# Three-pass projection in the second layer of block 1, with modulation chunks loaded elsewhere

## The chip, the cores and the metric

The kernel runs on one core of a Trainium2 chip, in float32. Its time is the device time of one launch in microseconds. TensorE is called PE here, VectorE DVE, ScalarE ACT and GpSimd POOL, as the profile's rows do; SP is the engine whose queue issues most DMAs.

## The reference

The model is two blocks in a row. What matters here is the first, which has two layers, each on 256 rows of context and 256 latent rows of width 1024:

```python
for l in range(DEPTH):
    mod_lat = silu_c @ w_ada[l] + b_ada[l]
    mod_ctx = silu_cc @ w_ada[l] + b_ada[l]
    x, ctx = _layer(x, ctx, mod_lat, mod_ctx, tabs, g_norm[l], w_in[l], ...)
...
xn = _rms_norm(x, g_norm) * (1 + sc[:, None]) + sh[:, None]
cn = _rms_norm(ctx, g_norm) * (1 + sc_c) + sh_c
(au, av, az, bq, bk, bv, bz, cq, ck, cv, co, cz, cg) = _split_proj(xn @ w_in)
```

`w_in` is 1024 x 3344 in each layer. Of the context the second layer needs only the columns of keys, values and gates. Behind the projection come a gated MLP branch, attention and an mLSTM, then `w_out`. The second block (a dilated attention, a forgetting attention, each with a mixture of experts) takes its own modulation from a vector, `mod = silu(c_2) @ w_ada_2[i] + b_ada_2[i]`, 6144 values for each of its layers. Those values depend on no row of x, so their weights (12 chunks of 512 columns, 2 MB each) may be used early: in block 1, where the kernel has room.

## The kernel before

**Weights.** All large weights pass through a ring of six buffers of 1 MB (`RING`, `SLOT`), filled by SP in the order of `ring_items()` (L96). A chunk of 512 columns is two items, one for each half of the 1024 rows. Item n goes where item n - 6 was, and SP waits for that one's last reader; it issues in order, so one item that cannot go yet holds all behind it.

**The projection** takes `w_in` in seven chunks of columns, `CHUNKS`: 272 columns first, then six of 512. There are four row tiles of 128 rows (0 and 1 context, 2 and 3 latent) and eight blocks of 128 along the 1024.

In the **first layer** `project_split` computes each product in three passes: the rows are kept as a rounded part `XH` and a remainder `XL`, the weights as `WH` and `WL`, and PE adds XH x WH, XH x WL and XL x WH (L3021 to L3023). POOL writes both weight parts, block by block (`WH` has four places, `WL` overwrites the ring's item). PE goes block by block over four tiles, so a chunk holds four PSUM banks until its last block; ACT then evicts them (`evict`, L2213), with a table load ahead where the chunk needs Gelu, Silu or Sigmoid. `MODS_BEHIND[0]` says which chunks of block 1's own modulation stand behind which chunk of the projection: PE multiplies them (`ada_rows`), DVE copies the result (`ada_copy`, L2354), PE gathers it into columns (`ada_row_cols`, L2936) and DVE adds the bias (`ada_sums`). While chunk 6 runs, PE does three pieces of side work, behind blocks 1, 3 and 5 (`SIDE_CHUNK`); each waits for a small write of DVE (`d2p`), the first for the one at L2645.

In the **second layer** `project` multiplies the rows `XT` by the ring's weights as they are (L3003), in full precision, tile by tile, 16, 256 or no columns for the context (`CTX_LAST`). `norm_by_tile` has PE wait for all eight blocks of XT before. Between the chunks DVE reduces seven chunks of the second block's modulation (3 to 9, `MODS_BEHIND[1]`): eight steps each on 128 x 512, L2321 and L2323, and PE turns each into columns with four small products (L2909). The work that follows a chunk (`post`: gates, the q/k norm, the layer norm of the values, the mLSTM's heads) is DVE's and ACT's, and starts when the chunk is evicted. Chunks 0 to 2 of that modulation come in the first layer's attention, 10 and 11 in the second's.

**Order.** All engines run their instructions in the order in which they are written; waits are on semaphores with constants.

## Time and profile before

| | us |
|---|---|
| median of three runs | 1531.93 |
| lowest and highest | 1531.39, 1532.83 |
| the profiled execution | 1527.17 |
| its span in the profile | 1525.3 |
| first layer's projection in the span | 30 to 212 |
| second layer's projection in the span | 387 to 508 |

The profile is of one execution. Busy time of an engine is the time in which an instruction of it ran; PE's matmuls are pipelined, so a record of 0.39 us may start 0.23 us behind the one before it, and the distance of the starts is what a matmul costs. A full precision matmul shows as two records. Times in rows are us from the span's start.

### The profile page before, as it was taken

Reading aid. Unit: us, or ns where it says so; the run is one execution under the profiler, and the core shown is the slowest. Engines: PE = TensorE matmul, PEld = TensorE weight load, DVE = VectorE, ACT = ScalarE, POOL = GpSimd, SP = SyncE. Lnnn points to the kernel's source line nnn. Section 1 sums busy time; section 2 is a strip of 40 time slices with the busy share of each in tenths; the row PEclk is TensorE's granted clock in tenths of the full one; section 3 lists DMA queues with packets and bytes.
Section 4 is the critical chain, followed back from the end, with each engine's and each line's share of the span. In section 5 each row is a group of like instructions: output and inputs, shape, how many; then the busy total and the mean of one; then the engine's idle time right before and its main releaser. Section 6 shows DMA issues by size and latency. Waiting matters only on the chain.

```text
span 1525.3 us, 19937 instructions
## 1 busy us (share of the span) xinstructions
PE 1460.2 (96%) x7623; PEld 1075.2 (70%) x7623; DVE 986.1 (65%) x1629; ACT 715.1 (47%) x1258; POOL 201.6 (13%) x232
## 2 busy tenths in 40 slices
PE   6999998999999899999999999999999999999998
PEld 3777773477655454788778877778886876778886
DVE  3326347683474864677677768688886656388786
ACT  4310228423312541655136533466675657367664
POOL 1656520224000010200220011000000005000000
PEclk8999999999999999999999999999999999999999
DMA  9674621203384531866687655099894440089892
GB/s 344 248 219 171 251 75 50 92 4 107 111 286 165 211 125 57 234 226 221 190 225 243 226 158 154 1 353 323 306 312 170 166 138 1 1 292 331 308 312 109
DMA packets 186475, 286.56 MB, mean 188 GB/s; under 512 B 13739, under 2 KB 95115, under 8 KB 186380
## 3 DMA queue, kind: packets, MB, share of 16 engines
q1 hardware_dynamic: 172080, 273.56, 52.5%
q0 software_dynamic: 13200, 8.84, 3.1%
q10 hardware_dynamic: 1100, 2.89, 0.5%
q8 instruction: 60, 0.98, 0.3%
q14 instruction: 35, 0.29, 0.1%
HBM read 283.77 MB, written 1.49 MB: 187 GB/s over the span
## 4 chain that ended last, share of the span: by engine, by line
PE 75%; DVE 13%; ACT 5%; DMA 3%; issue 1%; SPq 1%; POOL 0%; DVEq 0%; ACTq 0%
PE ps L1393 35%; PE ps L3003 9%; DVE WP L2278 4%; PE ps L2888 3%; DMA ring<-in_w_ada 3%; PE ps L3021 2%; PE ps L3022 2%; PE ps L3023 2%; PE ps L2900 2%; ACT ps L2159 2%; DVE P L2278 1%; PE ps L1708 1%; PE ps L2909 1%; PE ps L3109 1%; SPq L465 1%
## 5 line engine op out<-in xcount | busy, mean ns | idle before, releaser
L1393 PE MATMUL ps<-WB,YP 128*128 128x512 f32 x1196 | 287.9, 395 | 2.7 <-DVE WB L2278 2.7
L1393 PEld LDWEIGHTS ps<-WB,YP 128*128 128x128 f32 x1196 | 226.8, 191 | 50.7 <-issue 2.2
L2278 DVE TENSOR_TENSOR WP<-ring,WP 128x1024 fp32r<-128x1024 f32 (+1 forms) x196 | 228.0, 1199 | 47.3 <-ACT WP L845 46.3
L845 ACT ACTIVATE WP<-ring 128x1024 fp32r<-128x1024 f32 x188 | 190.8, 1053 | 53.3 <-PE ps L1393 53.1
L1393 PE MATMUL ps<-WP,XP 128*128 128x512 f32 x768 | 185.1, 393 | 1.5 <-DVE WP L2278 1.5
L2278 DVE TENSOR_TENSOR WB<-ring,WB 128x512 fp32r<-128x512 f32 x192 | 128.0, 690 | 84.8 <-ACT WB L696 83.0
L1393 PEld LDWEIGHTS ps<-WP,XP 128*128 128x128 f32 x768 | 142.0, 188 | 32.7 <-issue 1.9
L696 ACT ACTIVATE WB<-ring 128x512 fp32r<-128x512 f32 x192 | 114.1, 628 | 52.4 <-PE ps L1393 52.4
L3003 PE MATMUL ps<-ring,XT 128*128 128x512 f32 (+3 forms) x384 | 130.6, 497 | 1.1 <-ACT XT L2121 1.1
L2323 DVE SCALAR_TENSOR_TENSOR acc<-ring,silu_c,acc 128x512 f32<-128x512 f32 x168 | 127.0, 756 | 4.4
L2213 ACT ACTIVATE P<-ps 128x256 f32<-128x256 f32 (+2 forms) x68 | 27.3, 435 | 206.8 <-PE ps L3023 116.7
L1393 PE MATMUL ps<-WP,HP 128*128 128x512 f32 x480 | 115.7, 393 | 1.7 <-DVE HP L2278 1.1
L3003 PEld LDWEIGHTS ps<-ring,XT 128*128 128x128 f32 x384 | 69.7, 190 | 55.3 <-issue 49.3
L1393 PEld LDWEIGHTS ps<-WP,HP 128*128 128x128 f32 x480 | 89.2, 188 | 25.9 <-DVE HP L2278 7.6
L3021 PE MATMUL ps<-WH,XH 128*128 128x512 f32 (+1 forms) x224 | 86.0, 384 | 2.0 <-POOL WL L1963 1.0
L2900 PE MATMUL ps<-K 128*128 128x512 f32 (+3 forms) x232 | 82.6, 482 | 4.7 <-ACT GR L2253 2.0
L3022 PE MATMUL ps<-WL,XH 128*128 128x512 f32 (+1 forms) x224 | 84.2, 376 | 0.0
L3023 PE MATMUL ps<-WH,XL 128*128 128x512 f32 (+1 forms) x224 | 84.0, 375 | 0.0
L2520 DVE TENSOR_REDUCE small<-ps 128x2 f32<-128x256 f32 (+3 forms) x68 | 53.5, 786 | 44.4 <-PE ps L1686 18.5
L1963 POOL TENSOR_TENSOR WL<-ring,WH 128x512 fp32r<-128x512 f32 (+1 forms) x56 | 70.1, 1252 | 0.0
L2900 PEld LDWEIGHTS ps<-K 128*128 128x128 f32 x232 | 37.1, 197 | 27.4 <-issue 19.0
L763 ACT ACTIVATE E<-ps 128x512 f32<-128x512 f32 (+1 forms) x24 | 16.1, 670 | 85.7 <-PE ps L1722 44.0
(418 smaller groups left out, 2245.9 us busy)
## 6 DMA issues: line engine op xcount, KB each, us to landing
ring<-in_w_ada SPq DMA_DIRECT2D x72, 1024.0 KB, 7.4
ring<-in_a_w_in SPq DMA_DIRECT2D x36, 1024.0 KB, 5.1
ring<-in_w_gate SPq DMA_DIRECT2D x64, 512.0 KB, 4.8
ring<-in_w_up SPq DMA_DIRECT2D x64, 512.0 KB, 5.9
...
```

What stands on the lines that cost most here:

```text
L696: s_.activation(block_slot(q)[:, 0], w, ACT.Copy).then_inc(S("b_hi"), 1)
L845: s_.activation(WP[:, (m + 1) % CONV, 0, cols], slot(first + m)[:, cols], ACT.Copy).then_inc(S("w_hi"), 1)
L1393: ins = mm(dst, x(a), w(b), start=(start and n == 0), stop=(stop_ and n == 2))
L1963: nc.gpsimd.tensor_tensor(lo, w, hi.bitcast(F32), ALU.subtract).then_inc(S("win_lo"), 1)
L2278: return v.tensor_tensor(out_, a, b, op)
L2323: ins = v.scalar_tensor_tensor(o, w[:, kk, :], sc, o, ALU.mult, ALU.add)
L2520: ins = v.tensor_reduce(o[n], src, AX.X, ALU.max, negate=True)
L2900: mm(bank(b, at, at + cols), ones, K[:, 0:cols], start=True, stop=True)
L3003: ins = mm(b[:, 0:hi - lo], lhs(half * kk + k, t), w[:, k, lo:hi], start=(half == 0 and k == 0), stop=(half == len(its) - 1 and k == kk - 1))
L3021: mm(b, XH[:, k, cols], hi, start=(k == 0), stop=False)
L3022: mm(b, XH[:, k, cols], lo, start=False, stop=False)
L3023: ins = mm(b, XL[:, k, cols], hi, start=False, stop=(k == KB - 1))
```

## The change

1. The second layer uses `project_split` too. ACT writes `XH` and `WH` (`high_rows`, `high`), DVE `XL` and `WL` (`low_rows`, `low_weights`), four blocks ahead of PE, with a wait until PE has used the place. PE starts when four of the eight blocks of XT are there. DVE's work behind the chunks is cut into pieces that are dealt out by hand between the remainders (`second_layer_projected`); ACT's `post` stands inside the next chunk.
2. Of the seven modulation chunks in the second layer 8 and 9 stay. 3, 4 and 5 (`MODS_ASIDE`) are loaded in the first layer by ACT's DMA queue into one buffer of 1 MB of its own (`aside`), a half at a time: six loads, each but the first behind a wait for DVE. 6 and 7 (`MODS_BESIDE`) stand in the ring between and behind the two halves of the first layer's last weight chunk. DVE does their steps behind chunk 0, 1, 3 and 4; PE makes the columns behind chunks 2, 3, 5 and 6.
3. A ring item of the second layer's weights that is a first half is free when PE has used its fourth block, not at the end of the chunk.

```diff
-               {0: (('ada2', 0, 3),), 1: (('ada2', 0, 4),), 2: (('ada2', 0, 5),), 3: (('ada2', 0, 6),), 4: (('ada2', 0, 7),), 5: (('ada2', 0, 8),), 6: (('ada2', 0, 9),)})
+               {1: (('ada2', 0, 8),), 2: (('ada2', 0, 9),)})
+
+MODS_ASIDE = (3, 4, 5)
+MODS_BESIDE = (6, 7)
...
     for n in range(len(CHUNKS)):
         if n + 1 < len(CHUNKS):
             items.append(("win", 0, *CHUNKS[n + 1], 0))
+        if n == 5:
+            chunk("ada2", 0, MODS_BESIDE[0] * 512, MODS_BESIDE[0] * 512 + 512)
         for kind, layer, c in MODS_BEHIND[0].get(n, ()):
             chunk(kind, layer, c * 512, c * 512 + 512)
         if n + 1 < len(CHUNKS):
             items.append(("win", 0, *CHUNKS[n + 1], 1))
+        if n == 5:
+            chunk("ada2", 0, MODS_BESIDE[1] * 512, MODS_BESIDE[1] * 512 + 512)
...
+        aside = nc.alloc_sbuf_tensor_at("aside", [128, SLOT], F32, offset=pt_at + 4 * 1024)[:, :]
...
-        released, units, outs, dve_items, ada_items, mixed = [], 0, 0, 0, 0, 0
+        released, units, outs, dve_items, ada_items, mixed = [], 0, 0, 2 * len(MODS_ASIDE), 0, 0
...
-                    if it[1] == 0:
-                        released.append(("win_used", 7 * CHUNKS.index(it[2:4]) + 4))
-                        continue
+                    released.append(("win_used", 7 * (len(CHUNKS) * it[1] + CHUNKS.index(it[2:4])) + 4))
+                    continue
...
+        def ada2_acc(n):
+
+            if n <= 4:
+                return Qf[:, 4096 + 512 * (n % 2):4608 + 512 * (n % 2)]
+            return Ef[:, 1024:1536] if n == 5 else acc[:, n % 2, n // 2 % 2, :]
...
-            lo, hi = CHUNKS[q // 8]
+            l, n = divmod(q // 8, len(CHUNKS))
+            lo, hi = CHUNKS[n]
             w, k = hi - lo, q % 8
-            it = index[("win", 0, lo, hi, k // 4)]
+            it = index[("win", l, lo, hi, k // 4)]
             cols = slice((k % 4) * w, (k % 4) * w + w)
             return it, slot(it)[:, cols], WH[:, q % 4, 0:w], WL[:, it % RING, cols]
 
         def win_block_used(q):
 
-            return ("win_used", 7 * (q // 8) + q % 8 + 1) if q % 8 < 7 else ("proj", T * (q // 8 + 1))
+            return ("win_used", 7 * (q // 8) + q % 8 + 1) if q % 8 < 7 else released[win_block(q)[0]]
...
-                    pool.wait_ge(S("ada_cols"), 3)
+                    pool.wait_ge(S("ada_cols"), 8)
...
+            def load_aside(n):
+
+                if n > 0:
+                    act.wait_ge(S("dve_freed"), n)
+                ch, half = MODS_ASIDE[n // 2], n % 2
+                src = A["w_ada_2"][0, half * 512:half * 512 + 512, ch * 512:ch * 512 + 512].rearrange("(k p) n -> p k n", p=128)
+                act.dma_start(aside.rearrange("p (k n) -> p k n", k=4), src).then_inc(S("aside_full"), 16)
...
+                def high(q):
+
+                    it, w, hi_part, _ = win_block(q)
+                    if q % 4 == 0:
+                        item_ready(act, it)
+                    if q >= 60:
+                        name, value = win_block_used(q - 4)
+                        act.wait_ge(S(name), value)
+                    s_.activation(hi_part, w, ACT.Copy).then_inc(S("win1_hi"), 1)
...
+                    normalized_rows(range(T))
+                    act.wait_ge(S("mods_done"), 2)
+                    transposed_block(0, range(T), scale, shift)
+                    transposed_block(2, range(T), scale, shift)
+                    high_rows(0)
+                    high(56)
+                    high_rows(1)
+                    high(57)
+                    transposed_block(4, range(T), scale, shift)
+                    high_rows(2)
+                    high(58)
+                    high_rows(3)
+                    high(59)
+                    transposed_block(6, range(T), scale, shift)
+                    for k in range(4, KB):
+                        high_rows(k)
+
...
-                    norm(range(T), lambda s: A1[:, l, s, :], lambda s: M1[:, l, s, 0:8], mods=l + 1)
+                    second_layer_rows(lambda s: A1[:, 1, s, :], lambda s: M1[:, 1, s, 0:8])
                 for k, (lo, hi) in enumerate(CHUNKS):
+                    if l == 1:
+                        for j in range(7):
+                            if 8 * k + j < 52:
+                                high(60 + 8 * k + j)
+                            if (k, j) in ((1, 3), (3, 3), (5, 1)):
+                                post(1, k - 1, L)
...
-                    if k < 6:
-                        post(l, k, L)
+                    if l == 0 and k < 6:
+                        post(0, k, L)
+                    for n in ((1,), (2, 3), (4,), (5,), (), (), ())[k] if l == 0 else ():
+                        load_aside(n)
+                    if l == 1 and k < 6:
+                        high(67 + 8 * k)
...
+                    if l == 0 and ch in MODS_ASIDE:
+                        dve.wait_ge(S("aside_full"), 16 * (2 * MODS_ASIDE.index(ch) + half + 1))
+                        w = aside.rearrange("p (k n) -> p k n", k=4)
...
+                            o, sc = ada2_acc(a_), silu_c[:, col + k:col + k + 1]
...
+                        if k == SIDE_CHUNK[0] - 1:
+                            all_of(sums_and_gated_values(L))
+                        for ch in {0: MODS_ASIDE[0:1], 1: MODS_ASIDE[1:2], 3: MODS_ASIDE[2:3], 4: MODS_BESIDE}.get(k, ()):
+                            all_of(ada_ops("ada2", 0, ch))
+
+                def low_weights(q):
+
+                    _, w, hi, lo = win_block(q)
+                    dve.wait_ge(S("win1_hi"), q - 55)
+                    tt(lo, w, hi.bitcast(F32), ALU.subtract).then_inc(S("win1_lo"), 1)
...
+                    transposed_block(1, range(T), scale, shift)
+                    transposed_block(3, range(T), scale, shift)
+                    low_rows(0)
+                    low_weights(56)
...
+                def second_layer_projected(L):
+
+                    chunk_gates, heads_qk, rows_v, heads_m = gates(1), qk_norm(1), layer_norm_v(L), heads_of_mlstm()
+                    sums, mod8, mod9 = sums_and_gated_values(L), ada_ops("ada2", 0, 8), ada_ops("ada2", 0, 9)
+                    for k in range(len(CHUNKS)):
+                        for j in range(8):
+                            if j == 7:
+                                dve.wait_ge(S("evict"), c.up("evict", 4 if CTX_LAST[k] else 2))
+                            if 8 * k + j < 52:
+                                low_weights(60 + 8 * k + j)
+                            if k == 1:
+                                some(chunk_gates, (3, 2, 0, 0, 1, 0, 0, 0)[j])
+                                some(mod8, (0, 0, 1, 2, 1, 1, 1, 2)[j])
+                            if k == 2:
+                                some(mod9, 1)
+                            if k == 3:
+                                some(heads_qk, (4, 2, 3, 0, 1, 3, 1, 2)[j])
+                            if k == 4:
+                                some(heads_qk, 2)
+                            if k == 5 and j == 0:
+                                all_of(heads_qk)
+                                some(sums, 1)
+                            if k == 5:
+                                some(rows_v, (2, 1, 1, 0, 0, 0, 0, 0)[j])
+                                some(sums, (0, 0, 1, 0, 1, 2, 2, 1)[j])
+                                if j == 7:
+                                    for n in range(2):
+                                        columns_of("ada2", 0, 8 + n, bank(6 + n, 0, 8))
+                            if k == 6:
...
-                pe.wait_ge(S("xt_act"), c.up("xt_act", 4))
-                pe.wait_ge(S("xt_dve"), c.up("xt_dve", 4))
+                pe.wait_ge(S("xt_act"), c.up("xt_act", 4) - 4 + blocks)
+                pe.wait_ge(S("xt_dve"), c.up("xt_dve", 4) - 4 + blocks)
...
+            def project_split(l, n, behind):
+
+                lo_col, hi_col = CHUNKS[n]
+                tiles = []
+                for t in tile_order(l, n):
+                    r = (lo_col, hi_col) if (l == 0 or t >= 2) else CTX_LAST[n]
+                    if r:
+                        tiles.append((t, c.up("proj") - 1, slice(r[0] - lo_col, r[1] - lo_col)))
...
+                        pe.wait_ge(S("xt_lo"), KB * l + k + 1)
+                    if l == 0:
+                        pe.wait_ge(S("win_lo"), q + 1)
+                    else:
+                        pe.wait_ge(S("win1_lo"), q - 55)
+                    for t, u, r in tiles:
+                        if k == 0 and u >= 4:
+                            pe.wait_ge(S("evict"), u - 3)
+                        b, cols = bank(u % 4, 0, r.stop - r.start), slice(128 * t, 128 * t + 128)
+                        mm(b, XH[:, k, cols], hi[:, r], start=(k == 0), stop=False)
+                        mm(b, XH[:, k, cols], lo[:, r], start=False, stop=False)
+                        ins = mm(b, XL[:, k, cols], hi[:, r], start=False, stop=(k == KB - 1))
...
-                    if n == SIDE_CHUNK[0] and k in (1, 3, 5):
-                        behind[k // 2]()
+                    if n == SIDE_CHUNK[l] and k in ((1, 3, 5), (2, 4, 6))[l]:
+                        behind[(k - 1) // 2]()
...
+                    norm_by_tile(range(T), before_last=5, before_chunks=3, blocks=2)
...
+                    project_split(l, k, behind)
                     if l == 0:
                         if k > 1:
                             ada_row_cols([it[1:] for it in MODS_BEHIND[0][k - 2]])
+                        for n2 in {2: (0,), 3: (1,), 5: (2,), 6: (3, 4)}.get(k, ()):
+                            ada(1, bank(7, 128 + 8 * n2, 136 + 8 * n2))
                         for it in MODS_BEHIND[0].get(k, ()):
                             ada_rows(*it[1:])
-                    if l == 1 and k > 0:
-                        ada(1)
-                    if l == 1 and k == 6:
-                        ada(1)
+                    if l == 1 and k in (3, 4):
+                        ada(1, bank(3 + k, 0, 8))
```

Not shown: the yields that cut the work into pieces, the side work's places in the second layer (`SIDE_CHUNK` 5, now behind blocks 2, 4 and 6), and the columns' PSUM places.

DVE in the first layer, from the end of the work behind chunk 4 on (`acc<-ps` are the copies of `ada_copy`, `G` and `P<-P` begin the work behind chunk 5). Before:

```order
L2278 TENSOR_TENSOR P<-P,small 128x256 x4
L2354 COPY acc<-ps 128x512 x2
L2278 TENSOR_TENSOR M<-ps,VB 128x2x4 x2
L2282 TENSOR_SCALAR G<-G 128x2
L2282 TENSOR_SCALAR P<-P 128x4x256
L2511 COPY VX<-P 128x4x64
```

and now (`Q<-ring` and `E<-ring` are chunks 6 and 7):

```order
L2344 TENSOR_TENSOR P<-P,small 128x256 x4
L2391 TENSOR_SCALAR Q<-ring,silu_c 128x512
L2393 SCALAR_TENSOR_TENSOR Q<-ring,silu_c,Q 128x512 x7
L2391 TENSOR_SCALAR E<-ring,silu_c 128x512
L2393 SCALAR_TENSOR_TENSOR E<-ring,silu_c,E 128x512 x7
L2416 COPY acc<-ps 128x512 x2
L2344 TENSOR_TENSOR M<-ps,VD 128x4
L2344 TENSOR_TENSOR M<-ps,VB 128x2x4 x2
L2348 TENSOR_SCALAR G<-G 128x2
L2348 TENSOR_SCALAR P<-P 128x4x256
L2585 COPY VX<-P 128x4x64
```

Sixteen steps on the ring's items have come ahead of the copies, the sums and all that follows. In both, the small write that PE waits for in chunk 6 (MEMSET small, L2645 before) stands after the copies into `VX`.

ACT from the last transposed halves to the first eviction of the second layer. Before:

```order
L2090 ACTIVATE XT<-ps,M,A 128x256 x8
L2206 ACT_TABLE_LOAD
L2206 ACTIVATE small<-K 128x1
L2213 ACTIVATE P<-ps 128x256
L2213 ACTIVATE P<-ps 128x16 x2
```

and now:

```order
L2104 ACTIVATE XT<-ps,M,A 128x256 x2
L2236 ACTIVATE XH<-XT 128x512 x4
L2230 ACTIVATE WH<-ring 128x272 x4
L2230 ACTIVATE WH<-ring 128x512 x3
L2268 ACT_TABLE_LOAD
L2268 ACTIVATE small<-K 128x1
L2275 ACTIVATE P<-ps 128x256
```

Between the rows and the table load ahead of the first eviction there are now row parts (`XH`) and weight parts (`WH`), of which the last three belong to the next chunk.

DVE in the second layer, where the q/k norm begins. Before (`M<-ps` closes a modulation chunk):

```order
L2323 SCALAR_TENSOR_TENSOR acc<-ring,silu_c,acc 128x512 x7
L2278 TENSOR_TENSOR M<-ps,VD 128x4
L2278 TENSOR_TENSOR E<-P 128x128
L2435 TENSOR_REDUCE small<-E 128x2
L2278 TENSOR_TENSOR E<-P 128x128
L2435 TENSOR_REDUCE small<-E 128x2
L2278 TENSOR_TENSOR E<-P 128x640
L2435 TENSOR_REDUCE small<-E 128x10
L2278 TENSOR_TENSOR E<-P 128x640
L2435 TENSOR_REDUCE small<-E 128x10
L2436 MEMSET small 128x1
```

and now, in chunk 3 (`WL` are remainders of weights):

```order
L2344 TENSOR_TENSOR WL<-ring,WH 128x512
L2344 TENSOR_TENSOR E<-P 128x128
L2498 TENSOR_REDUCE small<-E 128x2
L2344 TENSOR_TENSOR E<-P 128x128
L2498 TENSOR_REDUCE small<-E 128x2
L2344 TENSOR_TENSOR WL<-ring,WH 128x512
L2344 TENSOR_TENSOR E<-P 128x640
L2498 TENSOR_REDUCE small<-E 128x10
L2344 TENSOR_TENSOR WL<-ring,WH 128x512
L2344 TENSOR_TENSOR E<-P 128x640
L2498 TENSOR_REDUCE small<-E 128x10
L2500 MEMSET small 128x1
```

The pieces of the norm stand between remainders, up to four of them in a row.

## Rows read from the trace of the kernel before

**Rows 1.** Page, section 1: busy us, share of the span, instructions.

```profile
PE 1460.2 (96%) x7623; PEld 1075.2 (70%) x7623; DVE 986.1 (65%) x1629; ACT 715.1 (47%) x1258; POOL 201.6 (13%) x232
```

**Rows 2.** Windows: length; busy us (instructions) of PE, PEld, DVE, ACT, POOL; clock; DMA.

```profile
387.00:508.00 121.00, 121.00 (x415) 70.94 (x414) 68.98 (x137) 23.69 (x46) 0.00 (x0) 1.00 0.59 209
30.00:212.00 182.00, 175.78 (x932) 136.22 (x932) 68.90 (x124) 35.20 (x69) 97.76 (x105) 1.00 0.61 209
```

**Rows 3.** PE's timeline, second layer's projection: start, us, line, what, count.

```profile
386.78 31.78 PE L3003 MATMUL ps<-ring,XT 128*128 128x272 f32 x128
...
419.22 13.98 PE L3003 MATMUL ps<-ring,XT 128*128 128x512 f32 x32
...
507.78 1.84 PE L2909 MATMUL ps<-K,acc 128*128 128x1 f32 x16
```

**Rows 4.** PE's timeline, passes of the first layer at 512 and 272 columns.

```profile
204.95 0.39 PE L3023 MATMUL ps<-WH,XL 128*128 128x512 f32 x1
205.18 0.39 PE L3021 MATMUL ps<-WH,XH 128*128 128x512 f32 x1
...
40.07 0.29 PE L3021 MATMUL ps<-WH,XH 128*128 128x272 f32 x1
40.19 0.29 PE L3022 MATMUL ps<-WL,XH 128*128 128x272 f32 x1
```

**Rows 5.** ACT's and DVE's timeline, and a page row of a remainder.

```profile
386.63 1.28 ACT L2206 ACT_TABLE_LOAD   x1
...
382.97 3.71 DVE L2402 TENSOR_SCALAR XT<-ps,A,M 128x256 f32<-128x256 f32 x8 [3.06 <-PE ps L2888]
...
L2278 DVE TENSOR_TENSOR WB<-ring,WB 128x512 fp32r<-128x512 f32 x192 | 128.0, 690 | 84.8 <-ACT WB L696 83.0
```

**Rows 6.** DVE's timeline, second layer: gates, a modulation chunk, the q/k norm.

```profile
398.16 0.23 DVE L2278 TENSOR_TENSOR small<-P,BG 128x64 f32<-128x64 f32 x1 [5.57 <-ACT P L2213]
...
404.03 5.47 DVE L2323 SCALAR_TENSOR_TENSOR acc<-ring,silu_c,acc 128x512 f32<-128x512 f32 x7
...
434.29 0.29 DVE L2278 TENSOR_TENSOR E<-P 128x128 f32<-128x128 f32 x1
...
442.16 1.02 DVE L2278 TENSOR_TENSOR P<-P,GQK 128x512 f32<-128x512 f32 x2
```

**Rows 7.** Timelines of ACT and its queue (ACTq) and of PE, first 62 us.

```profile
5.37 0.91 ACTq L2021 DMA_DIRECT2D X<-in_ctx  x2
...
19.23 1.06 ACT L2037 ACTIVATE P<-X 128x1024 f32<-128x1024 f32 x1 [0.87 <-DMA X<-in_x]
...
47.33 1.28 ACT L2206 ACT_TABLE_LOAD   x1
...
53.96 1.06 PE L2923 MATMUL ps<-ring,silu_c 128*32 128x512 f32 x8 [1.20 <-DMA ring<-in_w_ada]
```

**Rows 8.** Timelines of SP, POOL and DVE between chunks 5 and 6 of layer 1.

```profile
174.69 0.92 SPq L337 DMA_DIRECT2D ring<-in_w_in  x2
...
180.66 0.61 POOL L1954 CAST WH<-ring 128x512 fp32r<-128x512 f32 x1 [4.08 <-DMA ring<-in_w_in]
...
187.40 0.24 DVE L2278 TENSOR_TENSOR M<-ps,VB 128x8 f32<-128x8 f32 x2 [19.05 <-PE ps L2936]
...
190.58 0.06 DVE L2645 MEMSET small<- 128x1 f32 x1
```

**Rows 9.** Windows as in rows 2 for the ring's six transfers; five windows, three left out.

```profile
174.00:178.00 4.00, 4.00 (x19) 3.30 (x19) 0.00 (x0) 0.00 (x0) 1.85 (x2) 1.00 0.52 157
...
190.00:194.00 4.00, 4.00 (x24) 3.49 (x23) 0.86 (x6) 0.00 (x0) 2.93 (x4) 1.00 0.67 245
```

**Rows 10.** POOL's timeline in the first layer, with DVE beside it and alone.

```profile
118.29 1.87 POOL L1963 TENSOR_TENSOR WL<-ring,WH 128x512 fp32r<-128x512 f32 x1
...
181.23 1.29 POOL L1963 TENSOR_TENSOR WL<-ring,WH 128x512 fp32r<-128x512 f32 x1
```

**Rows 11.** Window as in rows 2, behind a gap of PE; the clock is 0.50.

```profile
380.00:382.00 2.00, 2.00 (x12) 2.00 (x11) 0.00 (x0) 1.09 (x1) 0.00 (x0) 0.50 0.00 0
```

178 lines of the change are left out of this document (103 added, 75 removed).

## The prediction

> **What bounds the kernel now.** I read the page's busy times first: TensorE (PE) is busy 96% of the span [rows 1]. Then the busy time by stretch: in the second layer's projection (387 to 508) PE is busy all 121 us, with VectorE at 69 and ScalarE at 24; in the first layer's (30 to 212) PE is busy 175.8 of 182, GpSimd 97.8 and VectorE 68.9 [rows 2]. Nothing is waited for in the second layer, so what its matmuls take is what it lasts. PE's own timeline gives that: full precision products from 386.78 on, and the last columns of a modulation chunk until 507.78 + 1.84 = 509.6 [rows 3]. That is 122.8 us for 96 products of 512 columns, 48 of 256, 16 of 272 and 16 of 16. The end of the program follows this stretch through a chain that is PE's nearly everywhere, so a microsecond saved here is one at the end, if no other is lost earlier.
>
> **Part 1: three passes instead of full precision.** A full product of 512 columns shows as two records, 13.98 us for 32 [rows 3], so 0.87 us. The first layer has the three-pass form already: starts at 204.72, 204.95, 205.18, so 0.2265 us a pass, and 0.125 us at 272 columns [rows 4]. Three passes: 0.68. PE's new work: 96 x 0.68 = 65.2; 16 x 3 x 0.125 = 6.0; 48 x 3 x 0.118 (272 scaled to 256) = 17.0; 16 x 3 of 16 columns at 0.08, an estimate between 0.06 and 0.125 = 3.8 (2.9 to 6.0). Sum 92.0. The sums and transposes at the side (2.2) and the two modulation chunks that stay (2 x 0.8) make 95.8. At full pace 122.8 - 95.8 = 27.0 is gained, five chunks' columns (4.0) being only moved, see part 3.
>
> **Part 2: who feeds the passes.** ScalarE writes 56 rounded parts (one input, shorter than what follows), VectorE 56 remainders of 0.69 [rows 5]; PE needs one pair per 1.36 us where two tiles run, so neither is the bound by that alone. The waits are at four places.
> Start: the transposed halves begin at 382.97 [rows 5]; two pairs of them, one row remainder and one weight remainder later it is about 386.5, and PE's first product stood at 386.78 [rows 3]. Nothing lost.
> Chunk 0: VectorE has eight transposed halves (3.7), eight row remainders (8 x 0.66) and five of the weights at 272 columns (5 x 0.4, scaled from 0.69) before PE can start block 4 [rows 5]: 382.97 + 3.7 + 5.3 + 2.0 = 394.0, with small waits for ScalarE 394.6. PE has done four blocks at 386.5 + 4 x 1.23 + 0.6 = 392.0: 2.6 lost, and the 0.6 on the way.
> Chunk 0 to 1: all four PSUM banks are used, and the first eviction stands behind a table load of 1.28 [rows 5], which stands behind the weight part that waits for PE's seventh block; with the eviction itself 1.4 lost.
> Chunk 3: VectorE has in chunks 1 to 3 24 remainders (17.3 with gaps), 16 modulation steps of 0.75 (12.0), the gates (ten small pieces at 0.23) and half of the q/k norm (7.8, from 434.29 to 442.16), all by [rows 6]: 39.4 us against PE's 16.5 + 10.9 + 10.9 = 38.3, with a lead of three blocks. 2.0 lost.
> Sum 6.6, with 0.4 for table loads at the other chunks 7.0. So the second layer gives 20 us (17 to 23: 16-column passes, and half or double the waits).
>
> **Part 3: the five modulation chunks in the first layer.** Their 5 x 0.8 us of columns on PE come in there, where PE is full: 4.0 lost. VectorE has idle time for the 40 steps, of which three chunks come on ScalarE's DMA queue. Of those six transfers five fall in gaps of the ring; the first is issued when the row parts end (47.3 [rows 7]), while six ring transfers run from 46 to 62 and PE waits for the third at 53.96. ScalarE's queue shares: the four X loads of 512 KB, issued from 5.37 on beside the ring, were waited for until 19.23, so 2.1 MB in 13.9 us, 150 GB/s [rows 7] where the ring alone moves about 390. So that wait grows by a transfer, 1 MB at 390 GB/s = 2.7 us (0 to 2.7, and up to 1.7 more if the clock falls). I take 2.7. ScalarE's waits for the buffer (until about 86 and 142) end before the next evictions (101.9, 153.8) and cost nothing; what hides them is PE's 21.8 us per chunk.
>
> The last two (6 and 7) are the point that decides. Behind chunk 4 VectorE takes their 16 steps **before** the copies, the work behind chunk 5 and the small write that PE waits for in chunk 6 behind block 1. Their four transfers stand in the ring between and behind the halves of the last weights. Before, the same six places start at 174.69, when half of chunk 5 is done; the first is in use by GpSimd at 180.66 [rows 8], and the rates, 157 GB/s in the stretch from 174, 387 to 400 in the three behind it and 245 in the last, add up to six transfers of 1.05 MB by 193.7 [rows 9]. So the sixth, the second half of chunk 7, is usable at 193.7 + 1.5 + 1.6 = 196.8 (1.5: the first one's transfer ends at about 179.1 and is used at 180.66; 1.6: two columns groups earlier on PE). Then four steps 3.0, two copies 1.4 and from the sums to the write 190.64 - 187.40 = 3.2 [rows 8], with 0.3 for the new sum: 204.7. PE comes to the wait at 187.2 + 3 x 0.8 + 2 x 2.72 = 195.0. **PE waits 9.7 us** (7 to 13). After a gap the clock is low: behind PE's gap of 2 us at 376 the stretch from 380 to 382 is at 0.50, the 1.2 GHz level [rows 11]. Some 3.4 us at it cost 1.7.
>
> The Trainium skill, *SBUF — State Buffer*, section "Who interferes with whom", says that GpSimd and VectorE share one port pair under an exclusive lock, so that one of them stands still for a whole instruction. By that the remainders of GpSimd would be late wherever VectorE's steps lie beside them; the rows show GpSimd's remainder at 1.87 at the longest against 1.29 [rows 10], which with its rounding of 0.6 still fits PE's 2.72 us per block.
>
> **Sum.** 20 gained; 4.0 + 2.7 + 9.7 + 1.7 = 18.1 lost: 1.9 us net. The profiled execution took 1527.17 (span 1525.3), so it would be 1525.2; on the median of the runs, 1531.93, it gives 1530.0.
>
> **Rivals.** (A) The sum above, 1530.0, own range 1525 to 1535.
> (B) No wait in chunk 6: the steps end before PE comes there. For it: VectorE has no work of its own from 168.4 to 186.3. Against it: it cannot take what has not arrived, and the last transfer's place is freed only when chunk 5 ends. Then 20 - 4 - 1.4 = 14.6 (0 to 2.7 of the first transfer): 1517.
> (C) Slower: VectorE becomes the bound of the second layer. With 39.4 us against 38.3 in chunks 1 to 3 it is already level; if each of these 24 blocks costs 0.3 us more in handing over (ScalarE, VectorE, PE in turn, over only four buffers), 7 more are lost, 13 stay, and with 18.1 lost it is 1537. It decides from 0.23 us a block on (5.5 us).
> (D) The lock's rule as a mechanism: GpSimd's pair of 1.9 us per block lengthened by two whole steps of 0.75 is 3.4, over PE's 2.72. Beside 40 steps (30 us, some 11 blocks) that costs up to 11 x 0.7 = 7 us: 1537. Against it: beside the q/k norm, which is denser, PE did not wait.
>
> **Numbers.** A 0.55, B 0.2, C 0.15, D 0.1. A measurement of this kernel tells about 0.2%, 3.1 us, from no change. Of A 0.22 is faster than that, 0.23 within and 0.10 slower; B is faster; C slower; D half within, half slower. Faster 0.42, within 0.28, slower 0.30. The range from 1518 to 1537 takes in most of each.
>
> **What would show it.** Right: second layer's passes 0.2265 apart, its projection about 103 us long, ending 20 us earlier relative to its start; a PE gap of 7 to 13 us in the first layer's chunk 6 that ends with VectorE's small write; the gap at 54 grown to about 4; PE gaps of 1 to 3 us in chunk 0, at its end and in chunk 3. Wrong: no gap in chunk 6 (B), remainders of VectorE as the releaser of most PE gaps of the second layer (C), gaps ended by GpSimd's remainders in the first (D).

## The result, and the profile after

Device microseconds, medians of the runs; the ratio is to the kernel before on the same chip, with its 95% interval.

| | median | range | profiled execution: span |
|---|---|---|---|
| before | 1532.63 | 1529.07 to 1537.25 | 1525.3 |
| after | 1542.75 | 1539.89 to 1553.3 | 1538.5 |

The ratio is 1.0082 [1.0054, 1.0110]: the change makes the kernel **0.8% slower**. (A ratio is taken over all runs and not from the two medians, whose quotient here is 1.0066.) Forecast were 1530.0 us and a range up to 1537, so it missed by 12.8 us.

The page of the changed kernel, section 1, to be read beside [rows 1]; then two windows, the first over the same 30 to 212 as in [rows 2], the second moved to where the second layer's projection now lies (length; busy us and instructions of PE, PEld, DVE, ACT, POOL; granted clock; DMA).

```profile
PE 1453.1 (94%) x7799; PEld 1103.5 (72%) x7799; DVE 1031.9 (67%) x1693; ACT 748.5 (49%) x1322; POOL 207.4 (13%) x232
...
30.00:212.00 182.00, 163.13 (x859) 125.12 (x857) 98.78 (x144) 32.72 (x64) 98.83 (x100) 0.95 0.69 238
411.00:522.00 111.00, 106.97 (x566) 92.18 (x565) 78.69 (x162) 58.28 (x110) 0.00 (x0) 0.94 0.47 161
```

From 30 to 212 TensorE is busy 12.7 us less, and the granted clock, 1.00 in both rows of before, is 0.95 and 0.94. PE's waits from 30 to 240 (us in total, times, longest) say where the first part went:

```profile
PE ps L3472 <- DVE small L2740: 9.4, 1, 9.4
PE ps L3090 <- DMA ring<-in_w_ada: 7.2, 3, 5.0
PE ps L3195 <- POOL WL L1977: 3.8, 1, 3.8
```

PE's timeline of the changed kernel at the places that the prediction named: behind the ring's transfer [rows 7], behind the weights at 104, behind VectorE's small write, the first attention transposes, the first and the last rows of the second layer's projection [rows 3], and in it block 4 of chunk 0 and the two waits of chunk 3.

```profile
56.45 1.93 PE L3090 MATMUL ps<-ring,silu_c 128*32 128x512 f32 x8 [5.03 <-DMA ring<-in_w_ada]
...
108.24 0.50 PE L3195 MATMUL ps<-WH,XH 128*128 128x512 f32 x1 [3.84 <-POOL WL L1977]
...
214.54 1.03 PE L3472 MATMUL ps<-small,K 128*128 128x16 f32 x4 [9.38 <-DVE small L2740]
...
241.03 1.17 PE L3055 MATMUL ps<-K,P 128*128 128x128 f32 x8
...
411.34 0.36 PE L3195 MATMUL ps<-WH,XH 128*128 128x272 f32 x1
...
418.66 0.36 PE L3195 MATMUL ps<-WH,XH 128*128 128x272 f32 x1 [1.51 <-DVE WL L2344]
...
467.77 0.51 PE L3195 MATMUL ps<-WH,XH 128*128 128x512 f32 x1 [0.66 <-DVE WL L2344]
470.21 0.50 PE L3195 MATMUL ps<-WH,XH 128*128 128x512 f32 x1 [0.77 <-DVE WL L2344]
...
522.00 0.60 PE L3055 MATMUL ps<-K,P 128*128 128x128 f32 x4
```

Four starts in PE's timeline cut each profiled execution into stages that can be compared: the first attention transposes of layer 1 (241.03 here, 214.07 before), the first product of the second layer's projection (411.34; 386.78), the transposes behind it (522.00; 509.49), and the end of the span.

| us | first layer's projection, up to | attention etc. | second projection | rest | span |
|---|---|---|---|---|---|
| before | 214.1 | 172.7 | 122.7 | 1015.8 | 1525.3 |
| after | 241.0 | 170.3 | 110.7 | 1016.5 | 1538.5 |
| difference | +27.0 | -2.4 | -12.1 | +0.7 | +13.2 |

Both numbers of the second projection, 12.1 and the forecast 20, count the columns of five modulation chunks that only moved to the first layer (4.0 by the prediction). The first column starts with the launch, and the start differs between executions: the first pass of the first layer's projection stands at 30.15 before, at 28.99 after and at 32.66 in the kernel with the spread steps (below).

```profile
30.15 0.59 PE L3021 MATMUL ps<-WH,XH 128*128 128x272 f32 x1
```

```profile
28.99 0.39 PE L3195 MATMUL ps<-WH,XH 128*128 128x272 f32 x1 [1.52 <-DVE XL L2344]
```

```profile
32.66 0.39 PE L3198 MATMUL ps<-WH,XH 128*128 128x272 f32 x1 [0.25 <-DVE XL L2344]
```

From there to the first attention transposes it took 183.9 us before and 212.0 after. The attention's -2.4 is no gain of the change either: the clock was at 0.50 for two stretches of 3.4 us there before (at 269.7 and 379.0) and for one after (at 241.9).

The second layer gave 12.1 where 20 were forecast; the first took 27.0 where 18.1 were. The waits account for part of that. Most of the rest is in the granted clock; here are windows of the changed kernel around the wait in chunk 6 and in the second layer's chunk 0 (columns as above):

```profile
205.00:214.50 9.50, 0.16 (x1) 0.00 (x0) 8.65 (x21) 0.00 (x0) 2.31 (x2) 0.64 0.00 0
214.50:224.50 10.00, 9.96 (x36) 8.29 (x37) 1.11 (x3) 0.00 (x0) 1.85 (x2) 0.66 0.01 2
...
411.00:419.00 8.00, 6.49 (x53) 6.12 (x52) 8.00 (x18) 7.00 (x17) 0.00 (x0) 1.00 0.09 14
419.00:433.00 14.00, 13.83 (x61) 13.18 (x60) 3.34 (x6) 4.85 (x12) 0.00 (x0) 0.51 0.40 139
433.00:447.00 14.00, 14.00 (x83) 12.34 (x82) 9.20 (x23) 7.86 (x13) 0.00 (x0) 1.00 0.25 80
```

From 419 to 433, and for 6.9 us behind the wait that ends at 214.54, TensorE runs at 0.50 (1.2 GHz) and is busy: each such microsecond does half a microsecond's work.

The third loss is on SyncE's queue. Its row loads (L465 before, L478 after) stand ahead of a weight half; first the queue before, then after (start, us, line, what).

```profile
77.45 0.51 SPq L465 DMA_DIRECT2D GH<-in_g_head  x1
...
79.59 0.77 SPq L465 DMA_DIRECT2D RW<-in_router_expert_w  x1
80.41 2.87 SPq L465 DMA_DIRECT2D WS<-in_w_s  x1
...
92.83 0.43 SPq L337 DMA_DIRECT2D ring<-in_w_in  x1
```

```profile
82.01 0.51 SPq L478 DMA_DIRECT2D GH<-in_g_head  x1
...
84.36 2.13 SPq L478 DMA_DIRECT2D RW<-in_router_expert_w  x1
86.53 3.81 SPq L478 DMA_DIRECT2D WS<-in_w_s  x1
...
100.51 0.52 SPq L345 DMA_DIRECT2D ring<-in_w_in  x1
```

The same 21 loads (the texts put on record say 22) hold the queue for 18.5 us instead of 15.4: ScalarE's third and fourth transfer (of six) are issued at 81.6 and 94.3, beside them. The half issued at 100.51 is what GpSimd, and then PE at 104.4, waits for. In the kernel without these transfers (below) the loads took 15.6 us again.

### The profile page after: what moved, and what is told of

Read it like the earlier page. It is cut to its first block, busy times and chain, and to the rows that moved or that the text cites. A ratio compares the mean times of both kernels' runs of the same rounds, so it can differ in the third digit from the quotient of the medians.

```text
span 1538.5 us, 20452 instructions
## 1 busy us (share of the span) xinstructions
PE 1453.1 (94%) x7799; PEld 1103.5 (72%) x7799; DVE 1031.9 (67%) x1693; ACT 748.5 (49%) x1322; POOL 207.4 (13%) x232
## 4 chain that ended last, share of the span: by engine, by line
PE 70%; DVE 16%; ACT 6%; DMA 4%; issue 2%; SPq 2%; POOL 0%; DVEq 0%; ACTq 0%
PE ps L1407 35%; DVE WP L2344 4%; PE ps L3195 4%; PE ps L3196 4%; PE ps L3197 4%; DMA ring<-in_w_ada 3%; PE ps L3055 3%; PE ps L3067 2%; PE ps L3170 2%; ACT ps L2173 2%; DVE P L2344 1%; SPq L478 1%; PE ps L1722 1%; PE ps L3076 1%; PE ps L3283 1%
## 5 line engine op out<-in xcount | busy, mean ns | idle before, releaser
L3195 PE MATMUL ps<-WH,XH 128*128 128x512 f32 (+3 forms) x400 | 152.1, 380 | 9.9 <-POOL WL L1977 3.8
L3196 PE MATMUL ps<-WL,XH 128*128 128x512 f32 (+3 forms) x400 | 148.8, 372 | 0.0
L3197 PE MATMUL ps<-WH,XL 128*128 128x512 f32 (+3 forms) x400 | 148.4, 371 | 0.0
L3195 PEld LDWEIGHTS ps<-WH,XH 128*128 128x128 f32 x400 | 79.8, 200 | 31.9 <-issue 8.5
L2393 DVE SCALAR_TENSOR_TENSOR acc<-ring,silu_c,acc 128x512 f32<-128x512 f32 x133 | 100.6, 756 | 2.8
L2275 ACT ACTIVATE P<-ps 128x256 f32<-128x256 f32 (+2 forms) x68 | 26.2, 438 | 134.7 <-PE ps L3197 133.5
L3197 PEld LDWEIGHTS ps<-WH,XL 128*128 128x128 f32 x400 | 79.3, 198 | 12.3
L3196 PEld LDWEIGHTS ps<-WL,XH 128*128 128x128 f32 x400 | 79.7, 199 | 11.2
L2615 DVE TENSOR_REDUCE small<-ps 128x2 f32<-128x256 f32 (+3 forms) x68 | 53.5, 786 | 45.2 <-PE ps L1700 18.5
L1977 POOL TENSOR_TENSOR WL<-ring,WH 128x512 fp32r<-128x512 f32 (+1 forms) x56 | 73.6, 1316 | 0.0
```

What stands on the lines that cost most here:

```text
L1977: nc.gpsimd.tensor_tensor(lo, w, hi.bitcast(F32), ALU.subtract).then_inc(S("win_lo"), 1)
L2393: ins = v.scalar_tensor_tensor(o, w[:, kk, :], sc, o, ALU.mult, ALU.add)
L2615: ins = v.tensor_reduce(o[n], src, AX.X, ALU.max, negate=True)
L3195: mm(b, XH[:, k, cols], hi[:, r], start=(k == 0), stop=False)
L3196: mm(b, XH[:, k, cols], lo[:, r], start=False, stop=False)
L3197: ins = mm(b, XL[:, k, cols], hi[:, r], start=False, stop=(k == KB - 1))
```

## The experiments

They are told in the order in which they ran; the first four take the changed kernel apart. W and K are the two theories of the first round: only the waits cost, or the low clock behind them costs as well.

**Products in the wait of chunk 6.**

```diff
 def sums_and_groups():
+    if l == 0:
+        keep_warm(10, 4)
     from_dve()
```

> The changed kernel, with ten products of 512 columns into a free PSUM bank put into TensorE's 9.4 us wait in chunk 6 of the first layer; nothing else waits for them. The wait stays, only TensorE is not idle in it. Theory W (only the waits cost, the low clock behind them would come anyway or costs nothing): the time of the changed kernel, 1542.8 us, within 1. Theory K (the gap lowers the granted clock, and that is a cost of its own): the stretch at 0.5 that reached 6.9 us past the gap's end goes, its work is done at full pace, 3.4 us are saved, 1539.3 us; the granted clock of the 10 us behind the wait is then 1.00.

Measured 1543.99 us, ratio to before 1.0077 [1.0051, 1.0103]: by the time alone no difference from the changed kernel, and W seems right. The profile says more. Windows of this kernel, in and behind the filled wait:

```profile
206.00:216.00 10.00, 10.00 (x30) 5.61 (x29) 9.54 (x15) 0.00 (x0) 5.01 (x4) 0.97 0.04 15
216.00:226.00 10.00, 9.15 (x43) 6.72 (x42) 3.51 (x14) 0.00 (x0) 2.32 (x3) 1.00 0.01 2
```

The stretch at 0.50 is gone, and from the end of the wait to the first attention transposes it takes 24.3 us instead of 26.5. But this execution has other low stretches (3.4 us more work time lost ahead of the wait, and 10 us in the part behind the second layer, which took 1026.8 us where it took 1016.5). So K holds at this place: 2.2 us are gained, and most of the missing part of the 3.4 is another stretch at 0.50, which begins here at 240.8, just ahead of the transposes, and costs 1.1. The total can't show it: low stretches elsewhere differ from execution to execution.

**The steps spread behind the small write.**

```diff
+steps = (op for ch in MODS_BESIDE for op in ada_ops("ada2", 0, ch))
+for n, _ in enumerate(sums_and_gated_values(L)):
+    some(steps, (2, 3, 2, 1, 1, 1, 1, 2, 0)[n])
+all_of(steps)
-all_of(sums_and_gated_values(L))
...
-4: MODS_BESIDE
```

> The changed kernel, with the 16 steps of the modulation chunks 6 and 7 on VectorE not ahead of the small write that TensorE waits for in chunk 6, but spread between the pieces of work that follow it. Their transfers and their places in the ring stay. The prediction's step for this wait (9.7 us, found 9.4) and nothing else: 1533.3 us. Theory K: the low clock goes with it, 3.4 us more: 1530.0 us. If the wait only moves to the columns of chunks 6 and 7 at the end of chunk 6 (the last transfer lands at about 195, the last step then ends at about 206, TensorE comes there at about 211), little is gained: over 1538.

Measured 1531.59 us, ratio 1.0020 [0.9994, 1.0045], 11.2 less than the changed kernel (9.5 by the two ratios), between the two numbers. No wait of PE for VectorE's small write is left; VectorE's timeline shows the write ahead of the first step:

```profile
203.88 0.06 DVE L2740 MEMSET small<- 128x1 f32 x1
203.97 0.49 DVE L2391 TENSOR_SCALAR Q<-ring,silu_c 128x512 f32<-128x512 f32 x1
```

The wait did not move to the end of chunk 6. The first stage takes 229.1 us, 12.0 less, although this execution started 3.7 later; from the first pass on it is 196.4 against 212.0, 15.6 less. Of these 9.4 are the wait and 3.4 the low clock behind it; the rest is less low clock at other places, which this edit does not touch.

**The first layer's part alone.** The second layer's lines of the kernel before are put back on all engines; on PE:

```diff
-project_split(l, k, behind)
+if l == 0:
+    project_split(0, k, behind)
+for t in tile_order(l, k) if l == 1 else ():
+    r = (lo, hi) if t >= 2 else CTX_LAST[k]
+    if r:
+        unit(lambda b: project(b, t, its, r[0] - lo, r[1] - lo, hi - lo))
```

> The first layer as in the changed kernel, the second layer's projection in full precision as before it, with its modulation chunks 8 and 9 behind its chunks 0 and 1. By the prediction's sum the second layer's passes give 20 us at the end: without them the changed kernel would take 1562.7 us. By the two traces (projection of 122.7 us before, of which 4 were moved columns, and 110.6 after) they give 12: 1554.8 us. The time over that of the kernel before, less the 4 us of columns that this leaves out of the second layer, is then what the first layer's part costs: 34 by the first, 26 by the second.

Measured 1554.0 us, ratio 1.0153 [1.0127, 1.0179], 11.3 more than the changed kernel. This looks like the 12 of the expectation, but both numbers in it are about 4 too high: the 20 and the 12 contain the moved columns, and in this run these stay in the first layer. Put right they are 16 (1558.7) and 8 (1550.7). The profile has the second one: the projection takes 118.3 us here and 110.7 in the changed kernel, 7.7 between them. The other 3.3 lie in the part behind it (1019.8 against 1016.5), where the program is the same and this execution had more stretches at 0.50. So the passes are worth 8 us by the traces and 11 by the medians, where the prediction had 16.

**The second layer's part alone.** Without `load_aside`, the four ring items and the steps:

```diff
-all_of(ada_ops("ada2", 0, ch))
+for _ in range(2):
+    to("dve_freed", v.memset(ada2_acc(a_), 0.0))
```

> The changed kernel without the ten transfers and the forty steps of the modulation chunks 3 to 7 in the first layer (two short writes of zeros in place of each chunk's steps; TensorE's columns stay). That part of the computation is left out, so its time tells only what the second layer's three passes and the five columns give by themselves. Sum of the waits alone (9.4 in chunk 6, 3.8 more for the third transfer of the ring at 51, 2.8 more for the weights at 104): 16.0 saved, 1526.8 us. Theory K (their low clock too: 3.4, 3.4 and 1.7): 24.5 saved, 1518.3 us. The prediction's own numbers (20 less 4): 1516.6 us.

Measured 1520.52 us, ratio 0.9931 [0.9907, 0.9955], 22.2 less than the changed kernel: more than the waits (16.0), near K's 24.5. This kernel leaves part of the computation out, so its time is no result. The first stage takes 217.8 us, 3.7 over before (4.3 from the first pass on), which is the columns. The second projection is 110.7 us as in the changed kernel: its loss comes from none of the first layer's transfers and steps.

**Why the clock falls in the second layer's chunk 0.** Three edits on top of the spread steps. Products in the wait of block 4:

```diff
     pe.wait_ge(S("xt_lo"), KB * l + k + 1)
+    if l == 1 and k == 4:
+        keep_warm(2, 4)
```

> On top of the kernel with the spread steps (1531.6 us; from the first pass of the second layer's projection to its end 110.8 us, with 13.7 us at a granted clock of 0.50 that begin in chunk 0's block 4 behind a wait of 1.5 us): two products into a free bank in that wait. Theory G (the gap of 1.5 us lowers the clock): the 13.7 us at 0.50 go or shrink to 3.4, the stretch takes 104 to 106 us, the kernel 1526. Theory N (the narrow passes of chunk 0, 272 and 16 columns behind a weight load each, don't hold the clock, gap or not): 110.8 and 1531.6, and the clock still falls in chunk 0.

Measured 1530.83 us, ratio 0.9994 [0.9977, 1.0011]; the second projection takes 105.8 us, with nothing at 0.50 in it. Wider passes for the context tiles:

```diff
+    r = (lo_col, hi_col) if n == 0 else r
     tiles.append((t, c.up("proj") - 1, slice(...)))
```

> On top of the kernel with the spread steps: in chunk 0 of the second layer the two context tiles' passes compute all 272 columns in place of the 16 that are used (the others are dropped), so that TensorE has more columns for each weight load; 48 passes grow from about 0.11 to 0.125 to 0.15 us, 1 to 2 us at full pace. Theory N (narrow passes don't hold the clock): the stretch at 0.50 shrinks from 13.7 to 3.4 us or goes, and the projection takes 105 to 108 us, the kernel 1527 to 1529. Theory G (the gap of 1.5 us does it): the stretch at 0.50 stays, and with the longer passes at half pace the projection takes 112 to 114 us, the kernel 1534.

Measured 1530.59 us, ratio 0.9992 [0.9966, 1.0018]; 106.1 us, nothing at 0.50 either. By the projection's time each theory is confirmed by its own edit. The kernel's time does not show it: 1526 and 1527 to 1529 were expected, and against the 1531.59 without these edits both are within 1 us, with overlapping intervals. The profiled executions spend 2.3 us more in the attention and 4 to 5.5 more behind the projection than that of the spread steps. In both executions, though, 3.4 us at 0.50 lay ahead of the projection (at 394), which the spread steps' execution did not have, so chance was a third explanation. Chunk 0 in full precision:

```diff
+if (l, k) == (1, 0):
+    for t in tile_order(l, k):
+        unit(lambda b: project(b, t, its, r[0] - lo, r[1] - lo, hi - lo))
...
-low_rows(0)
-low_weights(56)
...
+norm(range(T), scale, shift)
+for s_, value in used(index[("win", 1, *CHUNKS[0], 1)]):
+    dve.wait_ge(s_, value)
+for k in range(KB):
+    low_rows(k)
```

> On top of the kernel with the spread steps: chunk 0 of the second layer in full precision as in the kernel before (11.4 us there, from 386.78 to about 398.1, against 8 blocks of 1.40 = 11.2 in three passes at full pace), the other six chunks in three passes; VectorE rounds the remainders of the rows behind it, which TensorE waits about 1.3 us for. No narrow passes, no gap of 1.5 us in chunk 0. Both theories on the low clock expect it to go: 110.8 - 6.8 - 1.5 + 1.3 = 103.8 us for the projection, 1524.6 us for the kernel. If the clock falls all the same in chunk 1, whose passes are 512 and 256 columns, something else lowers it, and the kernel stays near 1531.

Measured 1537.3 us, ratio 1.0019 [0.9996, 1.0042]; the projection takes 109.4 us. The 13.7 us did not come, but a new wait did, and 6.8 us at 0.50 from within it:

```profile
PE ps L3180 <- DVE XL L2335: 5.6, 1, 5.6
```

The expected 1.3 us was wrong: as I had ordered it, VectorE takes all eight remainders of the rows (8 x 0.62) before the first of the weights.

**The transfers.** On top of the spread steps; first the wrong way:

```diff
+item_ready(act, index[("ada", 0, 2048, 2560, 1)])
 load_aside(0)
+load_aside(1)
```

> On top of the kernel with the spread steps: the first transfer on ScalarE's queue is issued when the ring's sixth transfer of the group around 51 us has landed (about 56) and not at 47, VectorE takes its steps ahead of chunk 0's evictions, so that the second transfer is over before SyncE's row loads from 77 on. The prediction's step on the ring (2.7 us, found 3.8), and the wait for the weights in chunk 2 that it did not have (2.8): waits for the third ring transfer back from 4.8 to 1.2, for the weights at 110 from 3.8 to 1.0: 6.4 saved, 1525.2 us; with the low clock behind them (3.4 and 1.7) 1520.1 us. If the row loads are slow for another reason than this transfer, only 3.6 to 5.3 are saved: 1526 to 1528.

Measured 1542.67 us, ratio 1.0078 [1.0049, 1.0108], a miss: chunk 0's evictions follow at 49 and not at 77, where I had taken them to be, and so stood behind the second load. PE's waits:

```profile
PE ps L3202 <- ACT P L2277: 14.2, 1, 14.2
PE ps L3097 <- DMA ring<-in_w_ada: 4.3, 4, 1.6
```

The second line answers the question all the same: the longest of the ring waits is 1.6, and the one that was 5.0 is 1.2 (at 54.25) when nothing is issued beside it. Then the row loads, five ring items later:

```diff
-EARLY_BEFORE, LATE_BEFORE = 10, 20
+EARLY_BEFORE, LATE_BEFORE = 10, 25
```

> On top of the kernel with the spread steps (1531.6 us): SyncE issues its 22 row loads five ring items later, behind the two weight halves, the two modulation halves and the next weight half that they stood ahead of. In the changed kernel the row loads took SyncE from 82.0 to 100.5 (18.5 us; 15.4 before, and 15.6 in the kernel without the first layer's transfers), and the weight half issued behind them is the one that TensorE waits 3.8 us for at 104. If that queue is the cause, the wait goes whole (before had 1.0 too): 3.8 saved and 1.7 for the low clock behind it, 1526.1 to 1527.8 us. If the ring's places are freed too late and not the queue, nothing changes: 1531.6.

Measured 1528.75 us, ratio 1.0000 [0.9975, 1.0026]. The time is 1 us over the forecast range, and its interval overlaps that of the spread steps, so the gain rests on the trace: the wait for the weights falls from 3.8 to 0.8 us, as the queue theory has it. The first stage takes 226.7 us, 2.4 less, of which 1.4 is an earlier start; this execution has 6.9 us more at 0.50 in it. And the first load behind chunk 0's evictions:

```diff
+if (l, k) == (0, 0):
+    item_ready(act, index[("ada", 0, 2048, 2560, 1)])
-for n in ((1,), (2, 3), (4,), (5,), ...)[k]:
+for n in ((0, 1), (2, 3), (4,), (5,), ...)[k]:
```

> On top of the kernel with the spread steps: the first transfer on ScalarE's queue is issued behind chunk 0's evictions and when the ring's transfer that TensorE waits for at 51 has landed. The run with the transfers behind, where the loads stood ahead of the evictions and held them up for 14.2 us, showed that ring wait at 1.2 again. Here no eviction waits: 4.8 to 1.2 in the ring wait, 3.6 saved, and 1.7 to 3.4 for the low clock behind it: 1524.6 to 1528 us. If the transfer costs its share of the ring wherever it lies (the ring moves its six halves from 46 to 62 at full rate), the time is lost at another ring wait: 1531.

Measured 1532.8 us, ratio 1.0015 [0.9992, 1.0037]. The ring wait is back at 1.2 (at 54.40), and the time is lost 50 us later:

```profile
PE ps L3199 <- POOL WL L1977: 7.7, 2, 7.4
```

From the first pass to the transposes it takes 197.8 us, 1.4 more than with the spread steps. So this repair gives nothing alone. SyncE issues the row loads from 77.9 to 97.6 here; those up to 83.9 take what they took before, and the slow ones stand beside ScalarE's third transfer, issued at 84.1 (the row of the expert weights 2.01 us, where it was 0.58).

**Together.** Spread steps, rows later, first load later, and the two products of block 4:

> The spread steps, the row loads later, the first load later, and the two products in the wait of chunk 0's block 4 in the second layer. Sum by the waits: 1531.6 - 3.8 - 3.6 = 1524.2 us; with the low clock behind them 1519 to 1521. For the clock in the second layer: where the stretch at 0.50 stands ahead of the projection (as in the two runs on top of the spread steps: at 394 in a program whose projection begins at 402) the projection takes 104 to 106 us, with or without these products; if it is the gap of 1.5 us that brings the 13.7 us at 0.50, it never comes here.

Measured **1521.25 us, ratio 0.9941 [0.9920, 0.9962]**: faster than both. The number came out as forecast, its parts did not. In the profiled executions the span is 8.5 us shorter than with the spread steps: 2.9 by an earlier start, 3.4 in the second projection (107.4), and only 2.1 in the rest of the first stage (194.3 from the first pass on), where 7.4 were expected for the two waits alone. Both of these waits are down (1.2 and 0.8 us), but three new ones for ring transfers stand at 134.7, 137.5 and 140.1, 2.8 us in all, with 6.8 us at 0.50 beside them. The same without the two products, but with nine products of 128 columns in the 2.0 us wait ahead of the projection:

```diff
+if blocks == 2 and t == tiles[-2]:
+    warm_blocks(4 + k % 4 for k in range(9))
 pe.wait_ge(S("xs"), c.up("xs"))
```

> As the kernel with three repairs, but with the products not in the wait of block 4; nine products of 128 columns stand in the 2.0 us that TensorE waits for the third tile of the second layer's norm, ahead of the projection. Theory P (one gap, that of 2.0 us some 9 us ahead of the projection, is what lowers the clock, and it depends on the run whether that shows at once, 3.4 us ahead of the projection, or only in chunk 0, where it lasts 13.7): neither stretch comes, the stretch from the first attention transposes to the end of the second layer's projection is 278.5 - 1.7 = 276 to 277 us, the kernel 1519 to 1521. Theory G or N (the gap in block 4, or the narrow passes): the 13.7 us at 0.50 in chunk 0 can come, 281 us, the kernel 1524.

Measured 1529.47 us, ratio 0.9991 [0.9968, 1.0014]; the two intervals don't meet. Of the 5.8 us between the two profiled spans 3.3 lie in the second projection, which is what the edit concerns, and 2.3 in the first stage, which it leaves alone. A window of this kernel in chunk 0, then one of the kernel with three repairs:

```profile
404.00:418.00 14.00, 13.69 (x59) 13.22 (x60) 3.80 (x7) 4.85 (x12) 0.00 (x0) 0.53 0.38 129
```

```profile
402.00:416.00 14.00, 12.60 (x81) 11.65 (x80) 5.49 (x15) 6.12 (x14) 0.00 (x0) 0.88 0.42 144
```

Theory P falls: the 2.0 us wait is filled and the low stretch comes all the same. Last, three that need no edit of a new kind: the wide passes (`r = (lo_col, hi_col)`) with the gap left in, `LATE_BEFORE = 25` in the kernel before, and the products in both waits.

> The spread steps, the row loads later and the first load later, no products in any wait of the second layer, and chunk 0's context passes 272 columns wide. In all eight kernels with the gap of 1.5 us in block 4 and narrow passes the 13.7 us at 0.50 came 8 us into the projection (110.7 us); in the two with products in that gap it did not. If the gap alone decides (G), it comes here too: projection 110.7 to 113 us, the kernel 1524 to 1527. If the narrow passes hold the clock down once it fell (N), the stretch is at most 6.8 us: projection 106 to 108 us, the kernel 1521.

Measured 1530.7 us, ratio 1.0006 [0.9973, 1.0038]; the projection takes 106.1 us at 1.00 throughout, as N had it, though PE waits 1.05 us in block 4 (with narrow passes it was 1.5). The median is far from N's 1521; its ten runs reach from 1520.0 to 1539.4, and the profiled one took 1523.4. PE's waits in block 4 and behind the eviction:

```profile
401.72 0.36 PE L3201 MATMUL ps<-WH,XH 128*128 128x272 f32 x1 [1.05 <-DVE WL L2346]
...
409.29 0.36 PE L3201 MATMUL ps<-WH,XH 128*128 128x256 f32 x1 [1.31 <-ACT P L2275]
```

> The kernel before, with the row loads five ring items later and nothing else. There TensorE waits 1.0 us for the weights at 100.85, and 1.5 and 1.6 us for ring transfers at other places. If what the repair gives is mostly the harm of the change undone, 1.0 us at most goes here, within 0.1% of the kernel before; if it is a gain of its own, 1527 or less.

Measured 1533.81 us, ratio 1.0025 [1.0005, 1.0046]: no gain there but a small loss, more than the 0.1% expected. The wait of 1.0 at 100.85 is gone, and two for ring transfers have come, 1.0 us at 131.3 and 1.5 at 133.9. What the later rows give in the changed kernel is harm of the change undone.

> The kernel with three repairs and the nine products of 128 columns in the 2.0 us wait for the third tile as well. Both waits of TensorE ahead of the second layer's chunk 1 are filled. By the low stretches of the runs so far nothing at 0.50 comes from 385 to 420: from the first attention transposes to the end of the projection 276 us against 277.7 in the run with three repairs, the kernel 1519.5 against 1521.3. If a low stretch elsewhere takes its place, no change.

Measured 1523.38 us, ratio 0.9952 [0.9926, 0.9977]. From the first attention transposes to the end of the projection it takes 277.7 us, as with three repairs, and not 276; the fourth adds nothing.

**What follows for chunk 0.** In all eight profiled kernels with narrow passes and the gap of 1.5 us, 13.7 us at 0.50 begin about 8 us into the projection, which takes 110.7 us. In none of the three with products in the gap (105.8, 107.4, 107.4 us) and in neither of the two with wide passes (106.1, 106.1) do they. Chance is an unlikely reading: two of these five had no low stretch ahead of the projection and the wait of 2.0 us there as it was, the same start as seven of the eight; the fifth, with that wait filled, is like the eighth. So with narrow passes it is the wait in block 4 that decides. That the narrow passes are needed as well is not shown as clearly: the wide ones come with a shorter wait, 1.0 to 1.05 us, and no run has wide passes with a wait of 1.5. Waits of that length elsewhere don't settle it, since the one of 1.55 us at 172.33 in the changed kernel has none at 0.50 behind it up to 190, and the one of 1.55 at 163.3 in the kernel before with later rows lies in 6.8 us at 0.50. Either edit is enough (two of the three with products had 3.4 us at 0.50 further on in the projection). In the projection the low clock costs 3.3 to 4.9 us and not the 6.8 of half of 13.7. At the low clock PE leaves ScalarE time: the eviction behind the table load is waited for 0.17 us in the changed kernel (at 428.9) and 1.3 to 1.4 where the clock stays up (the row at 409.29).

## Why the prediction was wrong

The table follows the prediction's sum. The measured column is from the profiled execution, against that of before.

| term | forecast | measured |
|---|---|---|
| first layer: five column groups | 4.0 | 4.9 |
| ring wait at 54 | 2.7 | 3.8 |
| wait for VectorE's small write | 9.7 | 9.4 |
| weights behind SyncE's row loads | not in the sum | 2.8 |
| low clock in the first layer | 1.7 | 9.0 |
| what is left over | 0 | -2.9 |
| sum | 18.1 | 27.0 |
| second layer's gain | 20 | 12.1 |

Of the last difference 1.2 is the earlier start and 0.8 less waiting at the other ring transfers; 0.9 stays open.

**The step that failed most is the clock term**, "Some 3.4 us at it cost 1.7". It was sized from one row, [rows 11], behind one gap of 2 us, and put at one place. The trace has four such places in the first layer: behind the ring wait (4.4 us of work at 0.50, 2.2 lost), behind the weights (3.4, 1.7 lost), behind the column groups at the end of chunk 5 (3.4, 1.7 lost) and behind the wait in chunk 6 (6.9, 3.4 lost). Three of them stand behind gaps that the change makes or lengthens; the prediction had the first as a bound ("up to 1.7 more if the clock falls") and left it out. The stretch behind those columns has no wait of PE ahead of it; it stands in the kernel without transfers and steps too, at 187.8, and in neither profile without these columns, but in several with them it is missing, so its cause is open. The 9.0 is the sum of one execution. The run with products in the wait shows the 3.4 behind that wait as caused by the gap (2.2 gained, 1.1 lost again to the stretch at 240.8), and the kernel without transfers and steps gives 22.2 us back where its waits are 16.0.

**Second layer, 20 against 12.** Forecast for the projection were 95.8 + 7.0 = 102.8 us, it took 110.7. The waits were foreseen well and a little too high: chunk 0 1.5 (2.6), chunk 3 1.4 (2.0), the eviction behind the table load 1.3 to 1.4 at full clock (1.4). What is late is 6.8 at the low clock; 1.4 in chunk 0, whose blocks take 1.40 (411.34 to 412.74) and not 1.23, since the three passes of 272 columns take 0.45 where narrow ones stand between; and 1.9 because the three passes of 512 columns take 0.70 on average and not 0.68. Of the 96 products the half beside 256 columns take 0.69 to 0.70 (504.64 to 505.34), those among their own kind 0.68, and eleven, most of them in and just behind chunk 3, take 0.76 to 0.86. So the 1.4 and less than half of the 1.9 are a pitch read in a stretch of one shape [rows 4] and used in one that mixes them; why the eleven are slow was not looked into. With the waits 3.0 lower, that leaves 0.8 open.

**The row loads.** "Of those six transfers five fall in gaps of the ring" looked at the ring's bytes, not at SyncE's queue, on which the next weights stood behind 21 loads. The prediction left out that a slower issue of the small loads puts off the weights behind them. The kernel with the rows later takes 3.0 of this 3.8 us wait away.

**Chunk 6: the right size, by luck.** The wait was forecast at 9.7 and is 9.4. But PE comes to it at 205.2 and not at 195.0, and the small write stands at 214.43 and not at 204.7: both sides are 10 us late, and the difference hides it. And the last transfer was to decide it, with four steps behind. VectorE never waits for one of them after the first (row at 192.32); its 16 steps take 17.4 us, 1.08 each and not 0.75:

```profile
192.32 1.18 DVE L2391 TENSOR_SCALAR Q<-ring,silu_c 128x512 f32<-128x512 f32 x1 [13.41 <-DMA ring<-in_w_ada]
193.54 7.72 DVE L2393 SCALAR_TENSOR_TENSOR Q<-ring,silu_c,Q 128x512 f32<-128x512 f32 x7
...
201.82 7.85 DVE L2393 SCALAR_TENSOR_TENSOR E<-ring,silu_c,E 128x512 f32<-128x512 f32 x7
```

**The rivals.** B (no wait in chunk 6) was wrong. C and D said 1537, nearer to the measured 1542.75 than A but still 5.8 below it. C's mechanism is wrong: VectorE's waits in the second projection sum to 2.9 us, and no block loses 0.3 steadily. D had the right pair of engines and the wrong victim (below). Of the forecast's chance of slower, 0.30, C and D gave 0.20 and the width of A 0.10; the clock had no rival of its own, and should have.
